# Half of the K pages in partition quadrants, transposed by VectorE in 32x32 blocks

## What is computed

```python
def sb_block(z, mask, v, carry):
    log_om = jnp.where(mask, jax.nn.log_sigmoid(-z), 0.0)
    suffix = lax.cumsum(log_om, axis=3, reverse=True) - log_om + carry[..., None]
    a = jnp.where(mask, jnp.exp(jax.nn.log_sigmoid(z) + suffix), 0.0)
    return jnp.einsum("bhqk,bkhd->bqhd", a, v.astype(jnp.float32)), carry + jnp.sum(log_om, axis=3)

def page_step(state, phys):          # newest page first
    o_acc, carry = state
    kp, vp = cache_k[phys], cache_v[phys]
    o_p, carry = sb_block(sb_logits(q, kp, sb_bias), True, vp, carry)
    return (o_acc + o_p, carry), None
```

## Time and profile before

| | us |
|---|---|
| median of the runs | 1237.78 |
| profiled execution | 1240.38 |
| its span, first to last instruction | 1238.7 |
| TensorE busy | 1130.0 |
| VectorE busy | 628.2 |
| ScalarE busy | 400.0 |
| GpSimd busy | 408.7 |

### The profile page before, as it was taken

How to read it: one execution, slowest core, us unless ns; L and a number is a source line. 1 busy time by engine, 2 the same in 40 slices (tenths; PEclk the granted TensorE clock), 3 DMA queues, 4 the chain that set the end, 5 groups by cost and what they waited for, 6 DMA issues and landing times.

```text
span 1238.7 us, 25950 instructions
## 1 busy us (share of the span) xinstructions
PE 1130.0 (91%) x9815; PEld 990.9 (80%) x9815; DVE 628.2 (51%) x853; ACT 400.0 (32%) x626; POOL 408.7 (33%) x341
## 2 busy tenths in 40 slices
PE   6679999989887899899979988899999999999997
PEld 2358879867666677667769966899999999999996
DVE  0463633555434776557469654854555002554444
ACT  2532332324344554454452244322121111211111
POOL 0133443524322253324434102333433334342330
PEclk9879999989978999999989999899999999999999
DMA  9526685855899698989854131332222222322222
GB/s 363 176 87 241 223 314 199 315 173 202 283 349 340 217 332 309 342 282 348 262 208 157 35 118 54 103 103 68 71 90 60 94 93 72 98 68 75 64 64 76
DMA packets 126409, 220.69 MB, mean 178 GB/s; under 512 B 9935, under 2 KB 68564, under 8 KB 126308
## 3 DMA queue, kind: packets, MB, share of 16 engines
q1 hardware_dynamic: 103010, 146.10, 34.5%
q0 software_dynamic: 20480, 67.13, 15.6%
q10 hardware_dynamic: 2818, 6.13, 1.4%
HBM read 213.52 MB, written 5.80 MB: 177 GB/s over the span
## 4 chain that ended last, share of the span: by engine, by line
PE 75%; DVE 11%; DMA 5%; ACT 3%; issue 2%; SPq 1%; POOLq 0%; ACTq 0%; POOL 0%; DVEq 0%
PE ps L512 36%; PE ps L1552 14%; PE ps L1633 8%; PE ps L1658 4%; DMA k_page<-in_cache_sb_k 3%; PE ps L1690 3%; PE ps L1508 2%; PE ps L573 2%; DVE h_lo L417 2%; DVE r_sq L670 1%; DVE run L1333 1%; DVE r_sum L675 1%; DVE aw L1339 1%; DMA v_late<-in_cache_sb_v 1%; PE ps L1669 1%
## 5 line engine op out<-in xcount | busy, mean ns | idle before, releaser
L468 POOL TENSOR_TENSOR w_lo<-w_raw,w_hi 128x2048 fp32r<-128x2048 f32 (+3 forms) x49 | 192.9, 3938 | 395.7 <-ACT w_hi L445 359.7
L512 PE MATMUL ps<-h_hi,w_hi 128*128 128x288 f32 x832 | 179.9, 298 | 8.8 <-DVE h_lo L417 5.7
L512 PE MATMUL ps<-h_lo,w_hi 128*128 128x288 f32 x832 | 179.2, 297 | 0.0
L512 PE MATMUL ps<-h_hi,w_lo 128*128 128x288 f32 x832 | 178.9, 297 | 0.0
L1633 PE MATMUL ps<-cc,k_page 128*128 128x128 f32 x1024 | 147.3, 298 | 33.5 <-DVE kT L1306 12.8
L1633 PEld LDWEIGHTS ps<-cc,k_page 128*128 128x128 f32 x1024 | 123.1, 152 | 55.8 <-issue 35.3
L445 ACT ACTIVATE w_hi<-w_raw 128x2048 fp32r<-128x2048 f32 (+3 forms) x47 | 77.9, 1660 | 255.1 <-PE ps L512 227.2
L609 POOL DMA_DIRECT2D v_late<-in_cache_sb_v x168 | 90.3, 537 | 180.4 <-issue 108.8
L512 PEld LDWEIGHTS ps<-h_hi,w_hi 128*128 128x128 f32 x832 | 135.1, 190 | 9.8 <-issue 7.1
L1306 DVE COPY kT<-ps 128x512 f32<-128x512 f32 x128 | 87.8, 691 | 98.4 <-PE ps L1633 98.1
L512 PEld LDWEIGHTS ps<-h_hi,w_lo 128*128 128x128 f32 x832 | 135.1, 190 | 0.0
(11 more groups left out here) (253 smaller groups left out, 1849.2 us busy)
## 6 DMA issues: line engine op xcount, KB each, us to landing
k_page<-in_cache_sb_k SPq DMA_DIRECT2D x256, 256.0 KB, 5.2
v_late<-in_cache_sb_v POOLq DMA_DIRECT2D x168, 256.0 KB, 5.3
v_early<-in_cache_sb_v POOLq DMA_DIRECT2D x88, 256.0 KB, 4.8
mw_raw<-in_w_in SPq DMA_DIRECT2D x12, 1024.0 KB, 5.3
w_raw<-in_w_gate SPq DMA_DIRECT2D x11, 1024.0 KB, 5.3
w_raw<-in_w_up SPq DMA_DIRECT2D x11, 1024.0 KB, 5.3
w_s<-in_w_in SPq DMA_DIRECT2D x4, 1536.0 KB, 12.5
w_raw<-in_w_down SPq DMA_DIRECT2D x8, 768.0 KB, 4.4
```

The costliest lines, as they stand in the source:

```text
L468: return nc.gpsimd.tensor_tensor(w_lo[s][:, ks, :], w_raw[s][:, ks, :], w_hi[s][:, ks, :].bitcast(F32), ALU.subtract)
L512: op = nc.tensor.matmul(ps[:, 2 * t + hf, 0:b - a], weights[s][:, k, t * P:(t + 1) * P], x[:, k0 + k, a:b], start=begin and k == ks[0] and ...
```

## The change

Of the four pages of each sequence in a chunk, two go the old way: `k_page` has four slots, TensorE transposes four pages with two PSUM banks, ScalarE and VectorE copy two each. The other two pages of each sequence go to `k_quad`: each page lands in one quadrant of 32 partitions, token 32a+i at partition i, place a. VectorE transposes all four quadrants with two instructions of 128 x 1024, in 32x32 blocks, into `kTq`. There a head's 64 numbers are split into two blocks of 32, and each partition quadrant belongs to one sequence and one page. So the scores of these pages are 32 products that contract over 64 partitions (two sequences x 32 numbers), 128 columns each, four added up per head pair, with queries laid out to match in `q_blk` (16 more small copies per group). The scores now lie in columns 384 to 895 of banks 2 and 3. SyncE asks for the four natural pages first, then waits until VectorE has transposed the quadrants of the chunk before (`s_kqt`), then asks for the four quadrant pages. VectorE transposes right after its K copies. To make room, the running product is written in place over `om_s`, and the next sigmoids wait for its carry. The diff, cut to the changed lines:

```diff
@@ -137,17 +137,19 @@
         beta_s = at("beta_s", [SEQ], R_V + 10240)
-        om_s = at("om_s", [SEQ], R_V + 12288)
+        q_blk = at("q_blk", [2 * HEADS, 32], R_V + 12288)
         awT_s = [at(f"awT_s{i}", [4, P], off) for i, off in enumerate((R_W + 45056, R_R))]
         zeros = at("zeros", [32], region(128))
-        run_s = at("run_s", [SEQ + 1], region(2080))
+        om_s = at("om_s", [SEQ + 1], region(2080))
         o_pair = at("o_pair", [2, P], region(1024))
-        k_page = at("k_page", [8, CH], R_M)
+        k_quad = at("k_quad", [4, CH], R_M)
+        k_page = at("k_page", [4, CH], R_M + 8192)
         v_early = [at(f"v_early{i}", [1, CH], off) for i, off in enumerate(
...
         v_late = at("v_late", [V2, CH], R_H)
-        kT = at("kT", [2, HP, SEQ], R_W + 16384)
+        kT = at("kT", [2, HP, 2 * P], R_W + 16384)
+        kTq = at("kTq", [2 * HEADS, P], R_W + 24576)
@@ -256,7 +258,8 @@
                                               "rows", "rows_tr", "rows_copied")}
-        s_kp = [sem(f"k_pages{i}") for i in range(4)]
+        s_kp = [sem(f"k_pages{i}") for i in range(2)]
+        s_kq, s_kqt = sem("k_quadrants_loaded"), sem("k_quadrants_transposed")
         s_v1 = [sem(f"v_early_pages{i}") for i in range(V1 // 2)]
@@ -602,18 +605,30 @@
+        def page_of(eng, C, q):
...
+            n = 64 * (C // 8) + 32 * (q // 4) + 28 - 4 * (C % 8) + q % 4
+            return eng.value_load(ptb[0:1, n:n + 1], min_val=0, max_val=N_POOL - 1)
...
-            n = 64 * (C // 8) + 32 * (q // 4) + 28 - 4 * (C % 8) + q % 4
-            page = eng.value_load(ptb[0:1, n:n + 1], min_val=0, max_val=N_POOL - 1)
+            page = page_of(eng, C, q)
             eng.dma_start(slot, cache[0, bass.ds(page, 1)].rearrange("o p h d -> p o (h d)")).then_inc(loaded, 16)
...
-            for q in range(8):
+            for n in range(4):
                 if C:
-                    sp.wait_ge(s_ktr, 8 * C + q - 7)
-                load_page(sp, C, q, ck, k_page[:, q:q + 1, :], s_kp[q // 2])
+                    sp.wait_ge(s_ktr, 4 * C + n - 3)
+                load_page(sp, C, 4 * (n // 2) + 2 + n % 2, ck, k_page[:, n:n + 1, :], s_kp[n // 2])
+            if C:
+                sp.wait_ge(s_kqt, 2 * C)
+            for s in range(2):
+                for x in range(2):
+                    page = page_of(sp, C, 4 * s + x)
+                    r = 32 * (2 * x + s)
+                    sp.dma_start(k_quad[r:r + 32, :, :],
+                                 ck[0, bass.ds(page, 1)].rearrange("o (a i) h d -> i (o a) (h d)", a=4)).then_inc(s_kq, 16)
@@ -1019,19 +1034,22 @@
-                for q in range(0, 8, 2):
-                    if q == 0 and C:
+                for n in (0, 2):
+                    if n == 0 and C:
                         act.wait_ge(m_["score"], 9 * ((C - 1) // 8) + (C - 1) % 8 + 2)
-                    act.wait_ge(s_ktr, 8 * C + q + 1)
-                    nc.scalar.activation(kT[:, q // 4, :, (q % 4) * P:(q % 4 + 1) * P], tiled(ps[:, q % 3, :]),
-                                         ACT.Copy).then_inc(m_["k_copied_a"], 1)
+                    act.wait_ge(s_ktr, 4 * C + n + 1)
+                    nc.scalar.activation(kT[:, n // 2, :, 0:P], tiled(ps[:, 0, :]), ACT.Copy).then_inc(m_["k_copied_a"], 1)
...
                 act.wait_ge(m_["score"], S + 1)
-                act.wait_ge(m_["weight"], S)
-                nc.scalar.activation(beta_s[:, 0:w], ps[:, 3, 0:w], ACT.Sigmoid, scale=SB_SCALE,
+                if S:
+                    G, k = divmod(S - 1, 9)
+                    act.wait_ge(m_["run"], 19 * G + 3 + 2 * k)
+                scores_ = ps[:, 2:4, :].rearrange("p b n -> p (b n)")
+                scores_ = scores_[:, SEQ:SEQ + w] if w == NS else scores_[:, 3 * P:7 * P]
+                nc.scalar.activation(beta_s[:, 0:w], scores_, ACT.Sigmoid, scale=SB_SCALE,
                                      bias=bias_s[:, 0:1])
-                nc.scalar.activation(om_s[:, 0:w], ps[:, 3, 0:w], ACT.Sigmoid, scale=-SB_SCALE,
+                nc.scalar.activation(om_s[:, 0:w], scores_, ACT.Sigmoid, scale=-SB_SCALE,
                                      bias=bias_s[:, 1:2]).then_inc(m_["om"], 1)
@@ -1244,6 +1262,7 @@
             step(dve, nc.vector.memset(q_bd[:, :, :, :], 0.0))
+            step(dve, nc.vector.memset(q_blk[:, :, :], 0.0))
             dve.wait_ge(s_rs, 2)
@@ -1299,31 +1318,38 @@
             def copy_k(C):
-                for q in range(1, 8, 2):
-                    if q == 1 and C:
+                for n in (1, 3):
+                    if n == 1 and C:
                         dve.wait_ge(m_["score"], 9 * ((C - 1) // 8) + (C - 1) % 8 + 2)
-                    dve.wait_ge(s_ktr, 8 * C + q + 1)
-                    nc.vector.tensor_copy(kT[:, q // 4, :, (q % 4) * P:(q % 4 + 1) * P], tiled(ps[:, q % 3, :]))\
-                        .then_inc(m_["k_copied_d"], 1)
+                    dve.wait_ge(s_ktr, 4 * C + n + 1)
+                    nc.vector.tensor_copy(kT[:, n // 2, :, P:2 * P], tiled(ps[:, 1, :])).then_inc(m_["k_copied_d"], 1)
...
+            def transpose_quadrants(C):
...
+                slots = kTq[:, :, :].rearrange("p b (a i) -> p a b i", a=4)
+                dve.wait_ge(s_kq, 64 * (C + 1))
+                for a in (0, 2):
+                    nc.vector.transpose(slots[:, a:a + 2, :, :], k_quad[:, a:a + 2, :].rearrange("p a (b j) -> p a b j", j=32))\
+                        .then_inc(s_kqt, 1)
...
                 if w == NS:
-                    nc.vector.memset(run_s[:, w:w + 1], 1.0).then_inc(m_["run"], 1)
+                    nc.vector.memset(om_s[:, w:w + 1], 1.0).then_inc(m_["run"], 1)
                     dve.wait_ge(m_["run"], R + 1)
                     R = R + 1
-                nc.vector.tensor_tensor_scan(run_s[:, 0:w][:, ::-1], om_s[:, 0:w][:, ::-1], om_s[:, 0:w][:, ::-1],
-                                             run_s[:, w:w + 1], ALU.mult, ALU.bypass).then_inc(m_["run"], 1)
+                om_ = om_s[:, 0:w][:, ::-1]
+                nc.vector.tensor_tensor_scan(om_, om_, om_, om_s[:, w:w + 1], ALU.mult, ALU.bypass).then_inc(m_["run"], 1)
                 dve.wait_ge(m_["run"], R + 1)
...
                     step(dve, nc.vector.memset(beta_s[:, NS:P], 0.0))
-                nc.vector.tensor_tensor(beta_s[:, 0:w], beta_s[:, 0:w], run_s[:, 1:w + 1], ALU.mult)\
+                nc.vector.tensor_tensor(beta_s[:, 0:w], beta_s[:, 0:w], om_s[:, 1:w + 1], ALU.mult)\
                     .then_inc(m_["weight"], 1)
                 dve.wait_ge(m_["weight"], S + 1)
-                nc.vector.tensor_copy(run_s[:, SEQ:SEQ + 1], run_s[:, 0:1]).then_inc(m_["run"], 1)
+                nc.vector.tensor_copy(om_s[:, SEQ:SEQ + 1], om_s[:, 0:1]).then_inc(m_["run"], 1)
                 dve.wait_ge(m_["run"], R + 2)
@@ -1354,6 +1380,17 @@
                 op.then_inc(m_["queries"], 1)
+                blocks = q_blk[:, :, :].rearrange("p (j h e) n -> p j h e n", h=2, e=2)
+                for s in range(2):
+                    for x in range(2):
+                        to = 32 * (2 * x + s)
+                        for h2 in range(2):
+                            for e in range(2):
+                                r = 64 * h2 + 32 * e
+                                op = nc.vector.tensor_copy(
+                                    blocks[to:to + 32, :, h2, e, 16 * s + 8 * h2:16 * s + 8 * h2 + 8],
+                                    pT[r:r + 32, T_Q:T_Q + HP, SEQ + 16 * G + 8 * s:SEQ + 16 * G + 8 * s + 8])
+                op.then_inc(m_["queries"], 1)
@@ -1376,6 +1413,7 @@
                         copy_k(C + 1)
+                        transpose_quadrants(C + 1)
                     if c == 7 and not last:
@@ -1422,6 +1460,7 @@
             copy_k(0)
+            transpose_quadrants(0)
             weights(0, 0, NS)
@@ -1577,7 +1616,7 @@
             def early_banks(C):
-                pe.wait_ge(m_["k_copied_d"], 4 * C + 3)
+                pe.wait_ge(m_["k_copied_d"], 2 * C + 2)
@@ -1623,14 +1662,12 @@
                 items_copied(max(C - 1, 0))
-                for q in range(8):
-                    pe.wait_ge(s_kp[q // 2], 32 * (C + 1))
-
-                    last = (q - 3) if q >= 3 else (6, 7, 5)[q] - 8
-                    if C or last >= 0:
-                        pe.wait_ge(m_["k_copied_a" if last % 2 == 0 else "k_copied_d"], 4 * C + last // 2 + 1)
+                for n in range(4):
+                    pe.wait_ge(s_kp[n // 2], 32 * (C + 1))
+                    if C or n >= 2:
+                        pe.wait_ge(m_["k_copied_d" if n % 2 else "k_copied_a"], 2 * C + n // 2)
                     for j in range(HP):
-                        op = nc.tensor.transpose(ps[:, q % 3, j * P:(j + 1) * P], k_page[:, q, j * P:(j + 1) * P], ident)
+                        op = nc.tensor.transpose(ps[:, n % 2, j * P:(j + 1) * P], k_page[:, n, j * P:(j + 1) * P], ident)
                     op.then_inc(s_ktr, 1)
@@ -1638,7 +1675,7 @@
```

(17 more changed lines are left out.)

## The result

The changed kernel takes 1280.35 us (median of four runs, 1278.79 to 1281.49); the kernel before takes 1238.55 us beside it. The ratio is 1.034, 95% interval [1.0318, 1.0362]: 42 us slower. The profiled execution took 1279.28 us with a span of 1277.6, 38.9 us more than the span of before.

A forecast was written before the change was run, and what follows sets the result against it. The early stage was taken as bound by TensorE, the late one by DMA and TensorE at almost the same level; 1240.4 - 7 early + 30 late = 1263 us profiled, so 1260 us measured, range 1226 to 1288 us.

The forecast's parts named there:

- TensorE, per chunk: Page transposes, scores and new products on TensorE: 6.02 us become 5.39 per chunk, a gain of 0.6 us.
- Early stage, -7 us: Chunks up to 12, bound by TensorE: 6.5 us from 11 chunks plus 0.5 us at the start, bounds -17 and +38.
- hidden: In early chunks VectorE's added transposes cost nothing, since TensorE needs 6.4 us for the tile in that gap.
- VectorE: Two transposes of 1.23 us replace two copies of 0.69: +1.1 us per chunk; scores wait +1.7 us in late chunks without tile.
- DMA per page: A page landing on 32 partitions holds the DMA engines 1.21 instead of 0.64 us: +0.57 us, +2.3 us per chunk.
- From DMA time to stage time: Late stage: 300 us of DMA time at a share of 0.95 make 316 us against 286, +30 us.
- The ring over the single k_quad buffer: Request, landing and transposes of quadrant pages take 9.3 to 11.9 us in a loop: takes slack, adds nothing to the DMA sum.
- Query copies: 16 small query copies added at 0.185 us each: 3 us, four times.
- (a): Rival: 32-partition loads cost nothing extra and VectorE's transposes become the wait: +2 us, 1240 us; chance 0.16.
- (b): Rival: loads cost nothing extra and transposes take 0.7 us each, so cheaper TensorE work wins: 1226 us; chance 0.17.
- (c): Rival: the 64-row products don't overlap and take 6 us per chunk: early +38, late at least +35, 1310 us; chance 0.04.
- (d): Rival: DMA-bound as forecast, but the late share doesn't rise: +49 instead of +30, 1280 us; chance 0.63 together with the forecast.

The follow-up runs named there:

- thin transposes: The changed kernel with VectorE's two 32x32-block transposes cut from 128x1024 to 128x32 from chunk 1 on: 1267.91 us, ratio 1.024 to the kernel before.
- wide_quads: The changed kernel with the four quadrant pages landing on 128 partitions each, same bytes, requests and waits: 1250.33 us, ratio 1.0107 to the kernel before.
- queries_first: The changed kernel with VectorE's query copies at a group's end ahead of its 32x32 transposes instead of behind: 1272.64 us, ratio 1.0285 to the kernel before.
- load_bench: The kernel before with five phases of page loads behind its end: 395 GB/s to 128 partitions, 236 to alternating quadrants, 210 to quadrants 0 and 32.
- before_quad_loads: The kernel before with only the second sequence's four K pages per chunk landing in 32-partition quadrants, asked for later: 1280.36 us, ratio 1.0342.

## Why the prediction was right, point by point

The direction and the main cause, the narrow landing, were right. The measured 1280 us lie inside the range, but 20 us above the 1260 that it named. Against the 1263 us for the profiled execution, 1279.3 were measured: 9.3 us of the difference lie in the early stage, 5.5 in the late one and 1.1 behind it. The terms:

- *TensorE, per chunk.* The new products were put at 1.88 us and take 1.50 at full clock, the halved scores at 0.96 and take 1.00. An early chunk won 0.8 us instead of 0.6. Right, a little too cautious.
- *Early stage, -7 us.* Measured +2.3 us up to chunk 12. The chunks gave 4.7 + 2.7 us as expected; the step that failed is "hidden" and "a gain of 0.5 us at the start". The boundary lost 6.3 us. The transposes were held against the tile of 6.4 us by themselves; with the query copies behind them, two of which took over 2 us, it is 10.8 us (236.38 to 247.18), longer than the tile. With thin transposes 6.0 us of the 6.3 are gone. The start lost 3.5 us. There the two transposes of chunk 0, 2.4 us, stand in the chain of waits, behind no tile; wide landings give back 1.8 us.
- *VectorE.* 1.23 us forecast for a transpose, 1.22 measured. The wait in front of the scores was forecast for late chunks without a tile, +1.7 us, and left out of the sum because DMA would hide it. The traces bear this out: 318.1 us for chunks 12 to 31 with the transposes and 318.0 with thin ones, though the medians leave room for some 4 us. It is hidden only as long as DMA is slow; with wide landings the same transposes cost 15.5 us.
- *DMA per page.* +0.57 us from the 64-partition rows; 0.45 us measured for the order in use. With 2.3 us per chunk the forecast was 300 us of DMA time; measured is 0.93 x 318.2 = 296 us, against 0.89 x 282.7 = 252 before. So the +44 us of the sum were met, but by luck. At 0.45 us the quadrant pages of 19 chunks make 34 us. The other 10 us are about what 19 of the 32 chunks take of the 16 us by which GpSimd's queue grew, and the prediction had no term for that: its V pages, same code and same bytes, hold the DMA engines longer beside narrow pages.
- *From DMA time to stage time.* The share was taken as 0.95 and is 0.93: 318 us instead of 316. With a base of 283 rather than 286 us (I had used windows, not the chunks' own times), +35.5 us instead of +30.
- *The ring over the single k_quad buffer.* It was said to take away slack and not to add. VectorE waited 27.4 us for quadrant pages, ten times; between 340 and 640 us it was 26.3 us in nine. wide_quads keeps the ring, with a faster landing, and there this wait is 8.3 us in three. A second buffer was not tried, so its share stays open.
- *Query copies.* Their own length was counted, 3 us four times, but no wait behind them at the group boundaries. At the two late ones TensorE waited 13.5 us for them, behind transposes that waited for their pages; queries_first gives some 7 us back.
- *Rivals.* (a), landing for free, is out by load_bench and by before_quad_loads. (b) is out by the 1.22 us of a transpose. (c) is out by 1.50 us for 32 products. (d), +49 at an unchanged share, was in time the closest: 1280. It met the total, but not by its reason: the share did rise, the late stage grew by 35.5 and not by 49 us, and the early stage, forecast at -7, came out at +2.3.

The signs named in advance came out: share 0.93 at a lower rate, quadrant pages as releasers of VectorE's transposes, shorter early chunks, longer landings. What the experiments add is the size of each: about 30 to 35 us the landing, 6 the transposes at the early boundary, 15 more in the late stage once the landing is fast, 7 to 8 back from TensorE, and some 7 that the order of queries and transposes costs at the late boundaries. These overlap and are not a sum.

## What to carry to other kernels

Before moving work off the busiest engine, cut the span into stages and look which resource is at its bound in each: here TensorE was busy for 8 us less in a stage that waited for DMA, and a layout made for an engine was paid for by the queue that fills it. Look at how many partitions a load reaches, and read GB/s beside the DMA share, since a slow landing looks just as busy. And where a change wins in one stage and loses in another, use it in the one.

## What the runs showed of the hardware

- Loads of 256 KB pages at a full DMA share: 395 GB/s to 128 partitions, 236 to 32 with alternating halves, 210 to 32 within one half.
- Narrow loads with wide ones of another queue beside them: 248 to 297 GB/s in the windows, but 36.7 us for 24 narrow and 12 wide pages, no less than the 34.6 us that they need one after the other.
- A transpose of 128 x 1024 fp32 in 32x32 blocks from SBUF to SBUF: 1.22 us. The plain copies of the earlier trace rows, carried on to 1024 elements, give 1.23 us.
- 32 products of 64 rows x 32 columns with 128 moving columns: 1.50 us, 47 ns each, less than the 59 ns of the V products with 128 rows; 2.62 us at the lower clock.
- Small VectorE copies from SBUF to SBUF of 0.17 us took 2.3 to 2.8 us in places, each ending with a subtraction of GpSimd; the cause was not separated.
